# Weights of a four-layer float32 program: split and released in halves of 1024 columns

## What is computed

```python
for i in range(2):                                  # first block
    h = rms_norm(x, ln_attn_g[i])
    dq, dk, dv, mq, mk, mv = split(h @ w_in[i])     # 6 x 512 columns
    y = concat(diff_attention(dq, dk, dv), moba_attention(mq, mk, mv))
    x = x + y @ w_out[i]
    u = causal_dwconv(rms_norm(x, ln_ffn_g[i]) @ w_up[i])      # 2 x 2816 columns
    g, up = split(u)
    x = x + (silu(g) * up) @ w_down[i]
for l in range(2):                                  # second block
    x = x + 0.5 * swiglu(rms_norm(x), ffn1 weights[l])         # 1024 -> 2 x 2816 -> 1024
    q, k, v, f, xr, gr, g_attn, g_rnn = split(rms_norm(x) @ w_in_2[l] + b_in_2[l])
    y_attn = forgetting_attention(q, k, v, log_sigmoid(f)) @ w_o_attn[l]
    y_rnn = (rg_lru(causal_conv(xr)) * gelu(gr)) @ w_o_rnn[l]
    x = x + (sigmoid(g_attn) * y_attn + sigmoid(g_rnn) * y_rnn) @ w_out_2[l]
    x = x + 0.5 * swiglu(rms_norm(x), ffn2 weights[l])
```

## Time and profile before

| | us |
|---|---|
| median of 3 runs (2121.68 to 2121.92) | 2121.69 |
| the profiled execution | 2121.57 |
| its span, first to last instruction | 2119.8 |
| TensorE busy | 1950.0 |
| VectorE busy | 1184.1 |
| ScalarE busy | 1070.4 |
| mean granted TensorE clock | 0.966 |

### The profile page before, as it was taken

One profiled execution on the slowest core, in us unless ns is written; L12 is line 12 of the kernel. 1 busy time (PEld: TensorE's weight loads), 2 busy tenths in 40 slices (PEclk: granted clock), 3 DMA queues, 4 the chain that ended last, 5 costly groups with the idle time before them and its releaser, 6 DMA issues.

```text
span 2119.8 us, 22469 instructions
## 1 busy us (share of the span) xinstructions
PE 1950.0 (92%) x9234; PEld 1618.1 (76%) x9234; DVE 1184.1 (56%) x1436; ACT 1070.4 (50%) x1278; POOL 38.1 (2%) x70
## 2 busy tenths in 40 slices
PE   6969999978999999996889999999999858999999
PEld 5757888856888788885668878888887746887888
DVE  5645767654767644545555654555444466565544
ACT  5645555654655544366555454454344745544442
POOL 2000000000000000000010000000000001000000
PEclk9989999989999999998899999999999979999999
DMA  7424555424555555543244745546554324355553
GB/s 230 139 80 139 188 190 179 145 94 139 160 198 179 179 180 195 181 132 107 90 156 141 229 159 183 194 159 199 182 191 131 119 93 159 129 174 167 187 183 115
DMA packets 156530, 337.62 MB, mean 159 GB/s; under 512 B 5799, under 2 KB 18556, under 8 KB 155916
## 3 DMA queue, kind: packets, MB, share of 16 engines
q1 hardware_dynamic: 153920, 327.57, 46.9%
q0 software_dynamic: 2048, 8.41, 1.3%
q10 hardware_dynamic: 459, 0.20, 0.0%
HBM read 335.09 MB, written 1.07 MB: 159 GB/s over the span
## 4 chain that ended last, share of the span: by engine, by line
PE 78%; DVE 10%; ACT 9%; issue 2%; DMA 1%; POOL 0%; SPq 0%; DVEq 0%; ACTq 0%; POOLq 0%
PE bank L404 24%; PE bank L406 23%; PE bank L405 23%; ACT w_hi L911 4%; DVE w_lo L1369 3%; ACT tmp L1063 1%; PE bank L506 1%; PE bank L458 1%; PE bank L788 1%; PE bank L552 1%; PE bank L594 1%; DVE tmp L1774 1%; DVE x L1408 1%; PE bank L641 1%; DMA raw<-in_w_in 1%
## 5 line engine op out<-in xcount | busy, mean ns | idle before, releaser
L1369 DVE TENSOR_TENSOR w_lo<-raw,w_hi 128x2048 fp32r<-128x2048 f32 x310 | 709.9, 2292 | 597.0 <-ACT w_hi L911 594.7
L911 ACT ACTIVATE w_hi<-raw 128x2048 fp32r<-128x2048 f32 x310 | 592.9, 1913 | 388.2 <-PE bank L406 387.6
L404 PE MATMUL bank<-w_hi,r_hi 128*128 128x512 f32 (+1 forms) x1792 | 694.0, 387 | 23.4 <-DVE r_lo L1396 11.4
L405 PE MATMUL bank<-w_lo,r_hi 128*128 128x512 f32 (+1 forms) x1792 | 682.7, 381 | 0.0
L406 PE MATMUL bank<-w_hi,r_lo 128*128 128x512 f32 (+1 forms) x1792 | 682.7, 381 | 0.0
L404 PEld LDWEIGHTS bank<-w_hi,r_hi 128*128 128x128 f32 x1792 | 342.1, 191 | 91.7 <-issue 15.0
L406 PEld LDWEIGHTS bank<-w_hi,r_lo 128*128 128x128 f32 x1792 | 340.5, 190 | 65.0
L405 PEld LDWEIGHTS bank<-w_lo,r_hi 128*128 128x128 f32 x1792 | 341.7, 191 | 61.0
L404 PE MATMUL bank<-w_hi,z_hi 128*128 128x512 f32 x656 | 261.7, 399 | 3.1 <-DVE z_lo L1369 3.1
L406 PE MATMUL bank<-w_hi,z_lo 128*128 128x512 f32 x656 | 256.8, 391 | 0.0
L405 PE MATMUL bank<-w_lo,z_hi 128*128 128x512 f32 x656 | 256.4, 391 | 0.0
(11 more groups left out here) (203 smaller groups left out, 1494.1 us busy)
## 6 DMA issues: line engine op xcount, KB each, us to landing
raw<-in_w_in SPq DMA_DIRECT2D x80, 1024.0 KB, 5.1
raw<-in_w_up SPq DMA_DIRECT2D x44, 1024.0 KB, 5.1
raw<-in_ffn_w_gate SPq DMA_DIRECT2D x44, 1024.0 KB, 5.1
raw<-in_ffn_w_up SPq DMA_DIRECT2D x44, 1024.0 KB, 5.0
raw<-in_ffn_w_down SPq DMA_DIRECT2D x44, 1024.0 KB, 4.9
raw<-in_w_down SPq DMA_DIRECT2D x22, 1024.0 KB, 5.0
raw<-in_w_out SPq DMA_DIRECT2D x16, 1024.0 KB, 5.0
raw<-in_w_o_rnn SPq DMA_DIRECT2D x8, 1024.0 KB, 5.0
```

The costliest lines, as they stand in the source:

```text
L404: pe.matmul(out_, lh, rh, start=start, stop=False, skip_group_check=True)
L405: pe.matmul(out_, lh, rl, start=False, stop=False, skip_group_check=True)
L911: A_(w_hi[:, s, :], raw[:, s, :], ACT.Copy).then_inc(hi_ready, 1)
L1369: return V.tensor_tensor(dst, src, hi.bitcast(F32), ALU.subtract)
```

## The change

`w_hi` and `w_lo` get six slots of half a unit (1024 columns) in place of three of a whole one, in the same memory. ScalarE and VectorE convert a unit in two instructions of 1024 columns, each with its own count of `hi_ready` and `lo_ready`. TensorE counts `part_done` up once for each half that it is through with, in place of `unit_done`, and ScalarE's copy of half n waits for half n - 6. `raw`, its DMAs and their three slots stay as they are. TensorE's order in the first half-unit of a chunk becomes: both t over the first two k, then both t over the last two; the hooks stand behind each of these. In the second half-unit the order stays, and the halves are reported in the run of t = 1. A down unit waits for each of its halves by itself.

```diff
@@ -22,7 +22,9 @@
 UNIT = 2048
 CW = 512
 STEPS = 6
+HALF = UNIT // 2
 NS = 3
+NH = 6
 EPS = 1e-6
 NEG = -1e30
 BUCKETS = 32
@@ -91,8 +93,8 @@
             return ctx.enter_context(nc.semaphore(name))
 
         raw = sb("raw", [P, NS, UNIT])
-        w_hi = sb("w_hi", [P, NS, UNIT], F32R)
-        w_lo = sb("w_lo", [P, NS, UNIT], F32R)
+        w_hi = sb("w_hi", [P, NH, HALF], F32R)
+        w_lo = sb("w_lo", [P, NH, HALF], F32R)
         x = sb("x", [P, TB, D])
         r_hi, r_lo = sb("r_hi", [P, KT, SEQ], F32R), sb("r_lo", [P, KT, SEQ], F32R)
         y_hi, y_lo = sb("y_hi", [P, KT, SEQ], F32R), sb("y_lo", [P, KT, SEQ], F32R)
@@ -172,7 +174,8 @@
 
 
         raw_full = [sem(f"raw_full{s}") for s in range(NS)]
-        hi_ready, lo_ready, unit_done = sem("hi_ready"), sem("lo_ready"), sem("unit_done")
+
+        hi_ready, lo_ready, part_done = sem("hi_ready"), sem("lo_ready"), sem("part_done")
 
         half_done = sem("half_done")
 
@@ -279,7 +282,7 @@
             def slot(u, src, rows):
                 s = u % NS
                 if u >= NS:
-                    sp.wait_ge(lo_ready, u + 1 - NS)
+                    sp.wait_ge(lo_ready, 2 * (u + 1 - NS))
                 sp.dma_start(raw[:, s, :].rearrange("p (k m) -> p k m", k=rows), src).then_inc(raw_full[s], 16)
 
             def cols(u, w, col, half):
@@ -408,26 +411,39 @@
             def nothing():
                 pass
 
-            def chunk_unit(u, half, banks, oh, ol, ready=None, free=None, hooks=(nothing, nothing), ends=True):
-
-                pe.wait_ge(lo_ready, u + 1)
-                s = u % NS
-                for t in range(TB):
-                    if free is not None and half == 0:
-                        free(t)
+            def chunk_unit(u, half, banks, oh, ol, ready=None, free=None, hooks=(nothing, nothing)):
+
+                def tile(t, kk):
+                    k = 4 * half + kk
+                    s, c = (2 * u + kk // 2) % NH, CW * (kk % 2)
+                    if ready is not None and t == 0:
+                        pe.wait_ge(rh_ready, ready + k + 1)
+                    return three(bank[banks + t][:, :], oh[:, k, t * P:(t + 1) * P], ol[:, k, t * P:(t + 1) * P],
+                                 w_hi[:, s, c:c + CW], w_lo[:, s, c:c + CW], k == 0, k == KT - 1)
+
+                if half == 0:
+
+                    for h in range(2):
+                        pe.wait_ge(lo_ready, 2 * u + h + 1)
+                        for t in range(TB):
+                            if free is not None and h == 0:
+                                free(t)
+                            tile(t, 2 * h)
+                            mm = tile(t, 2 * h + 1)
+                        mm.then_inc(part_done, 1)
+                        hooks[h]()
+                else:
+
+                    pe.wait_ge(lo_ready, 2 * u + 2)
                     for kk in range(4):
-                        k = 4 * half + kk
-                        if ready is not None and t == 0:
-                            pe.wait_ge(rh_ready, ready + k + 1)
-                        c = CW * kk
-                        mm = three(bank[banks + t][:, :], oh[:, k, t * P:(t + 1) * P], ol[:, k, t * P:(t + 1) * P],
-                                   w_hi[:, s, c:c + CW], w_lo[:, s, c:c + CW], k == 0, k == KT - 1)
-                    if t == 0:
-                        if half and ends:
-                            mm.then_inc(half_done, 1)
-                        hooks[0]()
-                mm.then_inc(unit_done, 1)
-                hooks[1]()
+                        mm = tile(0, kk)
+                    mm.then_inc(half_done, 1)
+                    hooks[0]()
+                    for kk in range(4):
+                        mm = tile(1, kk)
+                        if kk % 2:
+                            mm.then_inc(part_done, 1)
+                    hooks[1]()
 
             def chunk(u, banks, oh, ol, ready=None, free=None, h0=nothing, h1=nothing, h2=nothing, h3=nothing):
                 chunk_unit(u, 0, banks, oh, ol, ready, free, (h0, h1))
@@ -435,16 +451,18 @@
 
             def narrow_chunk(u, banks, free):
 
-                pe.wait_ge(lo_ready, u + 1)
-                s = u % NS
+                pe.wait_ge(lo_ready, 2 * u + 2)
                 for t in range(TB):
                     free(t)
                     for k in range(KT):
-                        c = 256 * k
+                        s, c = (2 * u + k // 4) % NH, 256 * (k % 4)
                         mm = three(bank[banks + t][:, 0:256], r_hi[:, k, t * P:(t + 1) * P],
                                    r_lo[:, k, t * P:(t + 1) * P], w_hi[:, s, c:c + 256], w_lo[:, s, c:c + 256],
                                    k == 0, k == KT - 1)
-                    mm.then_inc(half_done if t == 0 else unit_done, 1)
+                        if t and k % 4 == 3:
+                            mm.then_inc(part_done, 1)
+                    if t == 0:
+                        mm.then_inc(half_done, 1)
 
             def turn_x(where, n, half):
 
@@ -464,37 +482,35 @@
 
             def down_unit(u, f, j, half):
 
-                pe.wait_ge(lo_ready, u + 1)
                 pe.wait_ge(g_ready, 11 * f + 2 * j + half + 1)
-                s = u % NS
                 for i in range(2):
-                    tile = 4 * (j % 2) + 2 * half + i
+                    pe.wait_ge(lo_ready, 2 * u + i + 1)
+                    s, tile = (2 * u + i) % NH, 4 * (j % 2) + 2 * half + i
                     for t in range(TB):
                         for c in range(2):
-                            w = D * i + CW * c
                             mm = three(acc(t, c)[:, :], z_hi[:, tile, t * P:(t + 1) * P],
-                                       z_lo[:, tile, t * P:(t + 1) * P], w_hi[:, s, w:w + CW], w_lo[:, s, w:w + CW],
-                                       j == 0 and half == 0 and i == 0, False)
-                mm.then_inc(unit_done, 1)
+                                       z_lo[:, tile, t * P:(t + 1) * P], w_hi[:, s, CW * c:CW * (c + 1)],
+                                       w_lo[:, s, CW * c:CW * (c + 1)], j == 0 and half == 0 and i == 0, False)
+                    mm.then_inc(part_done, 1)
 
             def last_down(u, f, then):
 
                 j = STEPS - 1
-                pe.wait_ge(lo_ready, u + 1)
                 pe.wait_ge(g_ready, 11 * f + 2 * j + 1)
-                s = u % NS
+                pe.wait_ge(lo_ready, 2 * u + 2)
                 for c in range(2):
                     for t in range(TB):
                         for i in range(2):
-                            w, tile = D * i + CW * c, 4 * (j % 2) + i
+                            s, tile = (2 * u + i) % NH, 4 * (j % 2) + i
                             mm = three(acc(t, c)[:, :], z_hi[:, tile, t * P:(t + 1) * P],
-                                       z_lo[:, tile, t * P:(t + 1) * P], w_hi[:, s, w:w + CW], w_lo[:, s, w:w + CW],
-                                       False, i == 1)
+                                       z_lo[:, tile, t * P:(t + 1) * P], w_hi[:, s, CW * c:CW * (c + 1)],
+                                       w_lo[:, s, CW * c:CW * (c + 1)], False, i == 1)
+                            if (c, t) == (1, 1):
+                                mm.then_inc(part_done, 1)
                         if (c, t) != (1, 1):
                             mm.then_inc(half_done, 1)
                         if (c, t) == (1, 0) and then is not None:
                             turn_x(*then, 0)
-                mm.then_inc(unit_done, 1)
 
             def turn_prod(f, j):
 
@@ -904,11 +920,12 @@
             def hi(u):
                 if u >= UNITS:
                     return
-                s = u % NS
-                act.wait_ge(raw_full[s], 16 * (u // NS + 1))
-                if u >= NS:
-                    act.wait_ge(unit_done, u + 1 - NS)
-                A_(w_hi[:, s, :], raw[:, s, :], ACT.Copy).then_inc(hi_ready, 1)
+                act.wait_ge(raw_full[u % NS], 16 * (u // NS + 1))
+                for h in range(2):
+                    n = 2 * u + h
+                    if n >= NH:
+                        act.wait_ge(part_done, n + 1 - NH)
+                    A_(w_hi[:, n % NH, :], raw[:, u % NS, HALF * h:HALF * (h + 1)], ACT.Copy).then_inc(hi_ready, 1)
 
             def tick(u):
                 hi(u + 2)
@@ ScalarE, VectorE: chunk_wait, add_down
-                    act.wait_ge(unit_done, u_last + 1)
+                    act.wait_ge(part_done, 2 * (u_last + 1))
...
@@ -1371,9 +1388,11 @@
             def lo(u):
                 if u >= UNITS:
                     return
-                s = u % NS
-                dve.wait_ge(hi_ready, u + 1)
-                lo_part(w_lo[:, s, :], raw[:, s, :], w_hi[:, s, :]).then_inc(lo_ready, 1)
+                for h in range(2):
+                    n = 2 * u + h
+                    dve.wait_ge(hi_ready, n + 1)
+                    lo_part(w_lo[:, n % NH, :], raw[:, u % NS, HALF * h:HALF * (h + 1)], w_hi[:, n % NH, :]
```

(3 more changed lines are left out.)

## The result

| | before | after |
|---|---|---|
| median, us | 2121.68 | 2084.07 |
| lowest to highest | 2120.83 to 2121.92 | 2082.27 to 2085.99 |
| ratio, 95% interval | | 0.9824 [0.9807, 0.9841] |
| profiled execution, us | 2121.57 | 2085.99 |
| its span | 2119.8 | 2084.2 |

The kernel became 37.6 us (1.8%) faster; the forecast was 28 us, in a range of 2084 to 2110. The time lies 0.07 us inside the edge of that range, with executions on both sides of it, so that it lies inside is luck, and something was sized wrongly. The profiled execution of the changed kernel is its slowest, 3.7 us above its fastest, and the two traces differ by 35.6 us of span.

A forecast was written before the change was run, and what follows sets the result against it. Matmuls bound some stretches, a chain hopping between ScalarE and VectorE others. Savings of 16.7, 12.2, 1.4 and 0.8 less 0.9 and 0.2 gave 30.0 us, taken as 28: 2093.7 us, range 2084 to 2110.

The forecast's parts named there:

- The bound: Whole kernel: TensorE busy 92% of the span; any gain must come from the chain's 19% on ScalarE and VectorE.
- Prices: Start to start: w_hi 1.81 us, its half 0.95; w_lo 2.21, its half 1.14; splitting adds 0.09 and 0.07 us.
- part 1: Conversion in halves, so VectorE starts on the first half while ScalarE makes the second: 22 x 0.76 = 16.7 us saved.
- B place: One of 22 chain places where w_hi, then w_lo, precede VectorE work needing neither; 0.76 us saved each.
- The 2 us kept back: Held back from the sum in case ScalarE's own next step follows closely and a place returns less.
- Part 2, the release: TensorE reports each half when through, so VectorE reaches the additions into x 1.91 us sooner; 12.2 us saved at seven places.
- the four places: Where an attention or mixing output runs into a feed-forward: TensorE's idling of 2.87 us falls to about 0.96.
- the three: Between feed-forwards and into the mixing: TensorE's idling of 1.51 us before the transposes of x goes, 4.5 us together.
- the term of the clock: Less TensorE idling was to raise its granted clock behind the gaps: 1 us added, between 0 and 3.
- more than the sum: Rival, chance 0.10: full clock at 3 us, nothing held back, 6 us from early release; 2080 to 2088 us.
- Part 3 and 4: TensorE's new order in first-half units costs nothing, 0 to 3 us for banks; the weights' DMA wait, zero.
- The slower rival: Waits for the bank of t = 1, up to 1.36 us a chunk; 2135 us with 30 such chunks; chance 0.06.

The follow-up runs named there:

- the fillers: Kernel before the change plus 11 extra unused matmuls of 512 columns ahead of the wait for x at four places: 2113.5 us, ratio 0.9963.
- quarters: Changed kernel with conversions in instructions of 512 columns, releases still in halves: 2077.5 us, ratio 0.9797 to the kernel before.
- four moved lines: Changed kernel with VectorE doing normalise and logits before the conversion in block 1's softmax stretch: 2067.3 us, ratio 0.9749 to the kernel before.

## Why the prediction was right, and where it was short

**The bound.** Right. The feed-forward stretches kept their length to 0.1 us between their marks, and everything but the clock's part came from the chain's ScalarE and VectorE share.

**Prices, and part 1.** Right. 0.79 us a B place against 0.76, shown by the chain and by the whole kernel: with VectorE's subtraction undivided the gain is gone. The 2 us kept back were not needed, as recurrent and softmax stretches together gave 17.6 us against 16.7. In the softmax stretches the places did not show one by one: TensorE was not waiting at the first ones, and the sum of three appeared where it first did (2.4 us at one mark).

**Part 2, the release.** The mechanism was right, and the idling to 0.1 us at the four places and 0.2 us at the three: 13.1 us against 12.2. The step that failed is the term of the clock, "I add 1 us, between 0 and 3". It measured 6.4 us in the traces, and the fillers, which leave the wait as it was, gave the same 6.4 us at the same four places. I had taken the time of the eight transposes as the sign of a slow clock, and found two slow cases. But at the two places where they took 1.29 and 1.09 us the matmuls behind them were slow all the same (6 and 7 of them at 0.43 us). Reading on by a few rows would have shown all four, at 1.6 us each, and given 2121.7 - 33 = 2088 us.

**The clock elsewhere.** The rival "more than the sum", with a chance of 0.10, named the full clock as a cause and 2084 us as its likeliest time, and that is what was measured. Its reasons were right in part: it too had only 3 us for the clock, and the 6 us from early releases at B places did not come. The trace also lost 3.4 us, net, to slow stretches at other places than before, and without them the time would have been below the range. Such stretches are a second source of time that a sum over the chain does not hold, of either sign.

**Part 3 and 4.** Right: no wait for a bank appeared, and the old order measured the same. The slower rival has no support. What I can't explain is the rest of the 4.6 us that the kernel with whole conversions took more, beside the 0.8 us of a late DMA.

**The rule of fixed latency.** By the Trainium skill's figures (VectorE: DVE Perf Modes, The TRN2 errata), the split would have saved about 24 us, an estimate, if all of the fixed latency came on top. The rows decide against that reading: two w_lo of 1024 columns behind one another took 2.36 us where one whole took 2.29, and quarters, with twice as many instructions again, were faster still. The advice of the Trainium skill in Perfetto Trace Analysis (Optimizing Scalar/DVE Operations), to break instructions up where ScalarE and VectorE are not saturated but make others idle, is borne out: with VectorE's half of the split undone, the 37.6 us were gone.

## What to carry to other kernels

Where two engines hand a buffer on in series and both have time to spare, convert and release it in pieces: the pieces cost under 0.1 us each, and the saving is the shorter engine's time on all but one piece. But first ask why the conversion stands ahead of a critical step in an in-order queue at all; four moved lines gave here nearly half of what the split gave. And cost an idle gap of TensorE by the matmuls that follow it, too: look at the spacing of the next ten.

## What the runs showed of the hardware

- Behind idle gaps of 2.87 us (kernel before) all four times, behind gaps of 2.1 us (no early release) three times in four, and behind gaps of 2.0 us (only the copy in halves) two times in three, TensorE's granted clock was at the 1.2 GHz level, and 4 to 8 of its next matmuls of 512 columns lay 0.43 us apart instead of 0.23. Behind gaps of 1.51 us (kernel before, three times) and 0.89 us (kernel after, four times) it was at 2.4 GHz. Where it fell, the gap cost itself and about 1.6 us more.
- The length of a gap does not decide alone. At one place of the recurrent stretch the kernel before idles longer and keeps the clock (1.00 from 1089 to 1092 us), and the kernel after idles less and loses it (0.50 from 1070 to 1073 us): the same matmuls then take 0.64 us in place of 0.39. It is so in both layers, and costs 1.7 us each time. First before, then after:

```profile
1089.28 0.70 PE L613 MATMUL bank<-qk 128*128 128x256 f32 x2 [3.08 <-POOL tmp L397]
...
1090.46 0.39 PE L621 MATMUL bank<-qk 128*128 128x128 f32 x2
```

```profile
1068.98 0.70 PE L629 MATMUL bank<-qk 128*128 128x256 f32 x2 [1.90 <-POOL tmp L400]
...
1070.63 0.64 PE L637 MATMUL bank<-qk 128*128 128x128 f32 x2
```

- TensorE need not be idle for that. In both kernels, 48 matmuls of 8 columns follow each other without a gap in each layer of the second block. In the first of these layers of the kernel after, from about the 26th they lie 0.21 us apart instead of 0.11, and the clock stays low behind them although TensorE is busy all the time. The point moves: in the kernel before it is about the 35th in the first of the two layers and the 41st in the second, and in the second layer of the kernel after the spacing rises only behind the run. The first layer of the kernel after:

```profile
907.00:912.00 5.00, 5.00 (x22) 4.71 (x22) 0.54 (x3) 0.00 (x0) 0.00 (x0) 0.50 0.41 158
912.00:916.00 4.00, 4.00 (x11) 3.02 (x10) 0.00 (x0) 0.00 (x0) 0.00 (x0) 0.50 0.00 0
```
